# Halving the columns that each level of a triangular inverse multiplies, copies and merges, in a diffusion trunk with PEER experts on one core

## The chip, the core and the metric

One NeuronCore of a Trainium2 chip. The metric is the device time of one execution of the program in microseconds (us), where less is better. Durations below are us unless marked ns. The engines are PE (TensorE: MATMUL, with its weight loads LDWEIGHTS listed as PEld), DVE (VectorE), ACT (ScalarE), POOL (GpSimd) and SP (SyncE, which only issues DMAs here).

## The reference, cut to what matters

One inference step of two trunk layers, over 128 context tokens and 256 latent tokens. A layer has an input projection, four mixers side by side (a state space scan, a gated delta rule, a Fourier mixer, windowed attention), an output projection, and then PEER experts: every token picks 128 of 16,384 experts, and each expert is one row of 1,024 numbers in a table U and one in a table V, gathered from HBM.

The part that the change touches is the triangular solve of the gated delta rule:

```python
kk = jnp.einsum('bchid,bchjd->bchij', kc, kc)
A = jnp.where(strict, bc[..., :, None] * kk * decay, 0.0)
rhs = jnp.concatenate([vc * bc[..., None], kc * (bc * jnp.exp(gcum))[..., None]], axis=-1)
sol = lax.linalg.triangular_solve(jnp.eye(CHUNK, dtype=A.dtype) + A, rhs,
                                  left_side=True, lower=True)
```

All of it is fp32.

## The kernel before

**Tiles and units.** Tokens lie in three tiles of 128. The work is four units in this order: the context tile in layer 0 (one tile), the two latent tiles in layer 0, the context tile in layer 1, the two latent tiles in layer 1. Each unit runs its stages in a fixed order (norm, proj, intra for each tile, scan, fnet, attention, out, query, topk). The stage `st_intra(u, i)` holds the solve of one tile, so it runs six times: once, twice, once, twice.

**The inverse.** For each of two directions `d` (forward and backward) and four heads the kernel inverts a 128 x 128 unit triangular matrix by doubling. X and its transpose XT begin as the inverse of the 2 x 2 diagonal blocks. At level `lv` (1 to 6) blocks of 2^lv rows are joined to blocks of twice that size: P = N X (`inner`, L778), copied from PSUM to SBUF by ACT (L1284), then X gets the product of XT and P, and XT the product of P and XT (`outer`, L785), but only at the places that the level fills. The other places are kept by a mask: DVE merges the PSUM result into X (L1650) and XT (L1653) by `copy_predicated` under a mask of the level. The four heads of a direction share a PSUM bank of 512 columns: banks 0 and 1 take P, 2 and 3 X, 4 and 5 XT. At the last level X isn't needed, so it has no X product. The stationary operand (lhsT) of each of these matmuls is a 128 x 128 matrix; the moving operand is the second one. A helper `mm` (L565) issues every matmul and `tr` (L568) every transpose; `fn` (L1090) issues every ACT copy. An fp32 matmul appears in the trace as two LDWEIGHTS and two MATMUL instructions. The order on PE in a level is inner(0, lv), outer(1, lv-1), outer(0, lv), inner(1, lv).

**The weave.** Beside the units runs side work, at places written by hand (`SAMPLE_WEAVE`, `FIRST_WEAVE`, `PROMPT_WEAVE`, called by `gap`). In the first unit the side items are `modquad` (PE multiplies two of eight chunks of four weight blocks, which SP loads 1 MB at a time). In later units they are the experts of the unit before: for each of 128 slots POOL gathers 128 rows of a table with one indirect DMA (L542) into a ring of 12 places, and then either DVE multiplies and reduces it (`item_u`, L1967, table U) or PE sums it with weights (`item_v`, table V). An item is four such rows. POOL waits for a place of the ring to be free, DVE or PE wait for the row to land. In the latent units the six levels of an intra stage have items of the U kind between the merges of direction 0 and those of direction 1: one at each level of the first tile, and at all but one level of the second. In the context unit of layer 1 they have V items, two at each level. After the last unit the last experts run alone. The gathers go in one fixed order.

Of the kernel before, what the change touches and what calls it, by code (L numbers as in the profile page):

```python
# [27 lines left out]
P = 128  # L28
# [239 lines left out]
def build(nc, a, outs, seen):  # L268
# [11 lines left out]
    with ExitStack() as ctx:  # L280
# [5 lines left out]
        def sem(name):  # L286
            if name not in sems:
                sems[name] = ctx.enter_context(nc.semaphore(name))
            return sems[name]

        def tick(name, key=0, by=1):

            s = SEMAPHORE_OF.get(name, name)
            counts[s] = counts.get(s, 0) + by
            noted[name, key] = counts[s]
            return sem(s), by
# [25 lines left out]
        lvl = sb("lvl", [P, 2, LEVELS, P], mybir.dt.uint8)  # L322
# [68 lines left out]
        pb = ctx.enter_context(nc.psum_tensor("pb", [P, 6, 512], F32))  # L391
# [9 lines left out]
        def bc1(ap, n):  # L401

            return ap.unsqueeze(1).to_broadcast((ap.shape[0], n) + tuple(ap.shape[1:]))
# [14 lines left out]
        def big_at(o, *shape):  # L418
            n = int(np.prod(shape))
            v = big[:, o:o + n]  # L420
            if len(shape) == 2:
                return v.rearrange("p (a b) -> p a b", b=shape[1])
            if len(shape) == 3:
                return v.rearrange("p (a b c) -> p a b c", b=shape[1], c=shape[2])
            return v

        rows_in = [sem(f"rows_in{j}") for j in range(RING)]
        rows_used = [sem(f"rows_used{j}") for j in range(RING)]
        wcol_ready = sem("wcol_ready")
# [122 lines left out]
        def _(pe):  # L552
# [3 lines left out]
            def take(banks, until):  # L556


                for b in banks:
                    if b in held:  # L560
                        pe.wait_ge(*done(*held[b]))
                    held[b] = until

            def mm(out, lhsT, rhs, start=True, stop=True):
                return nc.tensor.matmul(out, lhsT, rhs, start=start, stop=stop)  # L565
# [169 lines left out]
            def st_intra(u, i):  # L735
                g, l, nt, NC, c0 = dims(u)
                t0 = slice(i * P, i * P + P)
                for d in range(2):
                    pe.wait_ge(*done("summands_ready", (u, i, d)))
                    take([2 * d, 2 * d + 1], ("dec_ready", (u, i, d)))  # L740
                    for m in range(2):
                        mm(pb[:, 2 * d + m, :], ones, big[:, d * 1024 + m * 512:d * 1024 + m * 512 + 512], stop=False)
                        for h in range(4):
                            last = mm(pb[:, 2 * d + m, h * P:h * P + P], ident, con("negm", d, P), start=False, stop=h == 3)
                    last.then_inc(*tick("rows_full", (u, i, d)))
                take([4, 5], ("cb_read", (u, i)))
                for gr in range(2):
                    s = slice(64 * gr, 64 * gr + 64)
                    last = mm(pb[:, 4 + gr, 0:P], cv[s, 2, t0], cv[s, 3, t0])
                last.then_inc(*tick("cb_full", (u, i)))  # L750
                gap(u, f"intra{i}", 0)
                for base, qk in ((0, 6), (2, 4)):
                    take([base, base + 1], ("kk_read" if base == 0 else "qk_read", (u, i)))
                    for h in range(HEADS):
                        s = slice(64 * (h % 2), 64 * (h % 2) + 64)
                        last = mm(pb[:, base + h % 2, h // 2 * P:h // 2 * P + P], cv[s, 6 + h // 2, t0], cv[s, qk + h // 2, t0])
# [8 lines left out]
                for h in range(HEADS):  # L765
                    for d in range(2):
                        last = mm(pb[:, 0, h * HD:h * HD + HD], big_at(2048 + 512 * d, 4, P)[:, h, :],
                                  big_at(3072 + 256 * d, 4, HD)[:, h, :], start=d == 0, stop=d == 1)
                last.then_inc(*tick("y_full", (u, i)))
                gap(u, f"intra{i}", 2)  # L770
                for d in range(2):
                    pe.wait_ge(*done("xt_ready", (u, i, d, 0)))
                    take([2 + d], ("x0_ready", (u, i, d, 0)))
                    for n in range(4):
                        last = tr(pb[:, 2 + d, n * P:n * P + P], big_at(2048 + 512 * d, 4, P)[:, n, :])
                    last.then_inc(*tick("x_full", (u, i, d, 0)))

                def inner(d, lv):  # L778
                    pe.wait_ge(*done("x_ready" if lv > 1 else "x0_ready", (u, i, d, lv - 1)))
                    take([d], ("p_copied", (u, i, d, lv)))  # L780
                    for n in range(4):
                        last = mm(pb[:, d, n * P:n * P + P], big_at(512 * d, 4, P)[:, n, :], big_at(1024 + 512 * d, 4, P)[:, n, :])
                    last.then_inc(*tick("p_full", (u, i, d, lv)))

                def outer(d, lv):  # L785
                    pe.wait_ge(*done("p_copied", (u, i, d, lv)))
                    pe.wait_ge(*done("xt_ready", (u, i, d, lv - 1)))
                    if lv < LEVELS - 1:
                        take([2 + d], ("x_ready", (u, i, d, lv)))
                        for n in range(4):  # L790
                            last = mm(pb[:, 2 + d, n * P:n * P + P], big_at(2048 + 512 * d, 4, P)[:, n, :],
                                      big_at(3072 + 512 * d, 4, P)[:, n, :])
                        last.then_inc(*tick("x_full", (u, i, d, lv)))
                    take([4 + d], ("xt_ready", (u, i, d, lv)))
                    for n in range(4):
                        last = mm(pb[:, 4 + d, n * P:n * P + P], big_at(3072 + 512 * d, 4, P)[:, n, :],
                                  big_at(2048 + 512 * d, 4, P)[:, n, :])
                    last.then_inc(*tick("xt_full", (u, i, d, lv)))

                for lv in range(1, LEVELS):  # L800
# [13 lines left out]
                for d in range(2):  # L814
                    for h in range(HEADS):
                        last = mm(pb[:, 0, d * 256 + h * HD:d * 256 + h * HD + HD],
                                  big_at(2048 + 512 * d, 4, P)[:, hpos(h), :], big_at(4096 + 256 * d, 4, HD)[:, h, :])
                last.then_inc(*tick("u_full", (u, i)))
                if g:
                    take([1], ("wt_copied", (u, i)))  # L820
                    for d in range(2):
                        for h in range(HEADS):
                            s = slice(64 * (h % 2), 64 * (h % 2) + 64)
                            o = d * 256 + h // 2 * P
                            last = mm(pb[s, 1, o:o + P], big_at(4608 + 256 * d, 4, HD)[:, h, :],
                                      big_at(2048 + 512 * d, 4, P)[:, hpos(h), :])
# [259 lines left out]
        def _(act):  # L1086
            step, stepped = stepper("act_step")

            def fn(out, in_, f=ACT.Copy, **kw):
                return nc.scalar.activation(out, in_, f, **kw)  # L1090
# [176 lines left out]
            def st_intra(u, i):  # L1267
                g, l, nt, NC, c0 = dims(u)
                gap(u, f"intra{i}", 0)
                for d in range(2):  # L1270
                    act.wait_ge(*done("rows_full", (u, i, d)))
                    for m in range(2):
                        for h in range(4):
                            c = m * 8 + d * 4 + h
                            last = fn(dec[:, d, m * 4 + h, :], pb[:, 2 * d + m, h * P:h * P + P], ACT.Exp, bias=sca[:, 10, i, c:c + 1])
                    last.then_inc(*tick("dec_ready", (u, i, d)))
                gap(u, f"intra{i}", 2)
                for d in range(2):
                    act.wait_ge(*done("x_full", (u, i, d, 0)))
                    fn(big_at(1024 + 512 * d, 512), pb[:, 2 + d, :]).then_inc(*tick("x0_ready", (u, i, d, 0)))  # L1280
                for lv in range(1, LEVELS):
                    for d in range(2):
                        act.wait_ge(*done("p_full", (u, i, d, lv)))
                        fn(big_at(3072 + 512 * d, 512), pb[:, d, :]).then_inc(*tick("p_copied", (u, i, d, lv)))  # L1284
                    gap(u, f"intra{i}", 2 + lv)
                act.wait_ge(*done("u_full", (u, i)))
                fn(sol[:, i, :, :], pb[:, 0, :].rearrange("p (a b) -> p a b", b=256)).then_inc(*tick("u_copied", (u, i)))
                if g:
                    act.wait_ge(*done("wt_full", (u, i)))
                    fn(solW[:, i, :], pb[:, 1, :]).then_inc(*tick("wt_copied", (u, i)))  # L1290
# [171 lines left out]
        def _(dve):  # L1462
# [3 lines left out]
            def item_const():  # L1466
                dve.memset(cinP[:, :, :], 0.0)
                dve.memset(cinS[:, :, :], 0.0)
                dve.memset(wcol[:, :, :], 0.0)
                dve.memset(c15[:, :], 15)  # L1470
                dve.memset(epsc[:, :], EPS).then_inc(*tick("init"))  # L1471

# [101 lines left out]
            def st_intra(u, i):  # L1574
# [11 lines left out]
                for d in range(2):  # L1586
                    b = bet[:, i, d * 4:d * 4 + 4].rearrange("p (pair par) -> p par pair", par=2)
# [15 lines left out]
                for d in range(2):  # L1603
                    dve.wait_ge(*done("dec_ready", (u, i, d)))
                    cb = pb[:, 4:6, 0:P]
                    for r in range(2):
                        dst = big_at(2048 + 512 * d, 2, 2, P)[:, :, r, :]
                        src = dec[:, d, 0:4, :].rearrange("p (g r) j -> p g r j", g=2)[:, :, r, :]
                        last = tt(dst, cb, src, ALU.mult)
                last.then_inc(*tick("cb_read", (u, i)))  # L1610
                dve.wait_ge(*done("qk_full", (u, i)))
                for d in range(2):
                    last = tt(attnT[:, i, d, :].rearrange("p (a b j) -> p a b j", a=2, b=2),
                              pb[:, 2:4, 0:256].rearrange("p a (b j) -> p a b j", b=2), heads_by_parity(dec[:, d, 4:8, :]), ALU.mult)
# [21 lines left out]
                for d in range(2):  # L1636
                    xt = big_at(2048 + 512 * d, 4, P)
# [3 lines left out]
                for lv in range(1, LEVELS):  # L1641
                    if lv == LEVELS - 1:
                        right_sides(u, i)
                    for d in range(2):
                        if d and lv < LEVELS - 1:
                            gap(u, f"intra{i}", 2 + lv)
                        x, xt = big_at(1024 + 512 * d, 4, P), big_at(2048 + 512 * d, 4, P)
                        if lv < LEVELS - 1:
                            dve.wait_ge(*done("x_full", (u, i, d, lv)))
                            dve.copy_predicated(x, bc1(lvl[:, 1 - d, lv, :], 4), pb[:, 2 + d, :].rearrange("p (a b) -> p a b", b=P)) \  # L1650
                                .then_inc(*tick("x_ready", (u, i, d, lv)))
                        dve.wait_ge(*done("xt_full", (u, i, d, lv)))
                        dve.copy_predicated(xt, bc1(lvl[:, d, lv, :], 4), pb[:, 4 + d, :].rearrange("p (a b) -> p a b", b=P)) \  # L1653
                            .then_inc(*tick("xt_ready", (u, i, d, lv)))
                gap(u, f"intra{i}", 1 + LEVELS)
                gap(u, f"intra{i}", 9)
# [403 lines left out]
```

## Time and profile before

| | |
|---|---|
| time, median of 3 runs (lowest to highest) | 2727.9 us (2726.73 to 2729.89) |
| the profiled execution | 2733.57 us |
| its span, from first to last instruction | 2731.8 us |
| mean granted TensorE clock over the span | 0.816 |
| busy: PE, PEld, DVE, ACT, POOL | 1789.8, 1096.3, 1645.4, 379.2, 1455.8 |
| HBM read | 955.11 MB, 350 GB/s over the span |
| indirect gathers on POOL | 1536 |

PE busy and PEld busy overlap, since a weight load runs beside the matmul before it. [...] An idle engine costs nothing by itself; what counts is which wait ends last in a stage. The span is cut by the view of stretches, where an x behind a busy time counts instructions that touch the stretch.

### The profile page before, as it was taken

The page shows a single profiled execution, that of the slowest core. Times are in us where ns is not written, and L with a number is a line of the kernel's source. Part 1 is how long each engine was busy: PE and PEld are TensorE (multiplying, and loading weights), DVE is VectorE, ACT ScalarE, POOL GpSimd, SP SyncE. Part 2 cuts the span into 40 slices and gives each one's busy share as a digit, 9 for nine tenths or more (in the row PEclk, how much of TensorE's full clock was granted, in tenths as well). Part 3 has the DMA queues.
Part 4 walks back from the last instruction along what each step waited for, and adds up shares of the span by engine and source line. Part 5 has one row for each costly group of instructions (what it writes and reads, how often), then busy time and mean ns, then how long its engine had stood idle before and what let it go on. Part 6 is the DMA issues. An engine that isn't in the chain of part 4 may idle for free. (4 is left out here: it accounts for less than half of the span.)

```text
span 2731.8 us, 28087 instructions
## 1 busy us (share of the span) xinstructions
PE 1789.8 (66%) x10274; PEld 1096.3 (40%) x10274; DVE 1645.4 (60%) x4093; ACT 379.2 (14%) x903; POOL 1455.8 (53%) x1540
## 2 busy tenths in 40 slices
PE   6988688768994111089888797767992000088888
PEld 5857567646643111054253386655650000011111
DVE  2526898871589898942116488882299999900000
ACT  3222231111111000011111132112110000000000
POOL 0000553332667676767765544333466777777775
PEclk9989798868996555589999898867996555599999
DMA  9487796656999999999999897656899999999998
GB/s 396 163 338 291 291 407 206 210 200 231 374 416 416 420 420 420 420 372 417 408 421 420 321 381 281 207 195 206 335 408 381 420 420 420 420 420 419 395 419 342
DMA packets 249208, 959.36 MB, mean 351 GB/s; under 512 B 32368, under 2 KB 33648, under 8 KB 231280
## 3 DMA queue, kind: packets, MB, share of 16 engines
q0 software_dynamic: 221184, 805.40, 74.6%
q1 hardware_dynamic: 19584, 142.62, 13.0%
q10 hardware_dynamic: 8304, 9.56, 1.0%
q8 instruction: 82, 1.34, 0.2%
q14 instruction: 54, 0.44, 0.0%
HBM read 955.11 MB, written 2.36 MB: 350 GB/s over the span
## 5 line engine op out<-in xcount | busy, mean ns | idle before, releaser
L542 POOL DMA_INDIRECT sb_ring<-in_peer_u,sb_idxu x768 | 726.6, 946 | 775.0 <-DVE sb_idxT L1935 287.7
L542 POOL DMA_INDIRECT sb_ring<-in_peer_v,sb_idxT x768 | 728.9, 949 | 478.7 <-PE pv L565 214.1
L1967 DVE CUSTOM_DVE_ANT_0 sb_ring<-sb_ring,pv 128x1024 f32<-128x1024 f32 x768 | 906.3, 1218 | 33.3 <-DMA sb_ring<-in_peer_u,sb_idxu 25.1
L565 PE MATMUL pv<-sb_ring,sb_wcol 128*32 128x512 f32 x3072 | 653.8, 626 | 74.8 <-DMA sb_ring<-in_peer_v,sb_idxT 63.0
L565 PE MATMUL pb<-sb_hT,sb_wring 128*128 128x256 f32 (+1 forms) x1920 | 375.6, 356 | 49.2 <-ACT sb_big L1090 26.7
L565 PEld LDWEIGHTS pb<-sb_hT,sb_wring 128*128 128x128 f32 x1920 | 321.5, 203 | 123.1 <-issue 70.0
L565 PEld LDWEIGHTS pv<-sb_ring,sb_wcol 128*32 128x32 f32 x3072 | 125.3, 111 | 541.7 <-DMA sb_ring<-in_peer_v,sb_idxT 365.5
L568 PE MATMUL pb<-sb_cst,sb_dots 128*128 128x128 f32 x6 | 2.4, 401 | 416.1 <-DVE sb_dots L1973 416.1
L565 PE MATMUL pb<-sb_big 128*128 128x128 f32 (+2 forms) x1888 | 244.9, 296 | 32.0 <-DVE sb_big L1650 22.7
L565 PEld LDWEIGHTS pb<-sb_big 128*128 128x128 f32 (+1 forms) x1888 | 233.1, 205 | 53.9 <-DVE sb_big L1650 29.7
L1981 DVE COPY sb_accv<-pv 128x512 f32<-128x512 f32 x12 | 8.3, 690 | 342.2 <-PE pv L565 337.7
L565 PE MATMUL pb<-sb_big,sb_cst 128*128 128x256 f32 (+6 forms) x304 | 100.2, 506 | 129.7 <-ACT sb_cinP L1090 45.0
L568 PEld LDWEIGHTS pb<-sb_cst,sb_dots 128*128 128x128 f32 x6 | 1.0, 160 | 418.1 <-DVE sb_dots L1973 418.1
L1090 ACT ACTIVATE sb_big<-pb 128x512 f32<-128x512 f32 (+3 forms) x184 | 84.1, 466 | 524.4 <-PE pb L565 442.6
L565 PEld LDWEIGHTS pb<-sb_big,sb_cst 128*128 128x128 f32 (+2 forms) x304 | 53.5, 231 | 148.9 <-ACT sb_big L1090 73.1
L565 PE MATMUL pb<-sb_wring,sb_hT 128*128 128x256 f32 x352 | 82.1, 392 | 26.7 <-DVE sb_cv L1512 26.7
L1836 DVE SCALAR_TENSOR_TENSOR sb_xT<-pb,sb_modT,sb_xT 128x128 f32<-128x128 f32 (+1 forms) x32 | 13.4, 417 | 137.5 <-PE pb L565 137.5
L1650 DVE COPY_PREDICATED sb_big<-sb_lvl,pb 128x512 f32<-128x512 uint8 x60 | 43.5, 726 | 83.4 <-PE pb L565 83.4
L1843 DVE MAX8 sb_xe<-sb_dec 128x8 f32<-128x128 f32 x128 | 27.9, 280 | 103.8 <-ACT sb_cv L1090 64.0
L565 PEld LDWEIGHTS pb<-sb_wring,sb_hT 128*128 128x128 f32 x352 | 68.8, 197 | 37.7 <-issue 28.0
L1090 ACT ACT_TABLE_LOAD x54 | 69.3, 1283 | 6.2 <-DVE sb_epsc L1471 3.7
L1967 DVE DVE_READ_ACCUMULATOR2_ANT sb_dots<- 128x1 f32 x768 | 63.6, 83 | 0.0
(234 smaller groups left out, 1662.3 us busy)
## 6 DMA issues: line engine op xcount, KB each, us to landing
sb_ring<-in_w_mod_blocks SPq DMA_DIRECT2D x38, 1024.0 KB, 8.2
sb_wring<-in_w_in_blocks SPq DMA_DIRECT2D x34, 1024.0 KB, 7.7
sb_wring<-in_w_q_blocks SPq DMA_DIRECT2D x26, 1024.0 KB, 8.5
sb_wring<-in_w_out_blocks SPq DMA_DIRECT2D x14, 1024.0 KB, 7.7
sb_ring<-in_peer_u,sb_idxu POOLq DMA_INDIRECT x768, 9.2
sb_ring<-in_peer_v,sb_idxT POOLq DMA_INDIRECT x768, 8.0
sb_wring<-in_w_mod_blocks SPq DMA_DIRECT2D x10, 1024.0 KB, 7.7
sb_ring<-in_w_in_blocks SPq DMA_DIRECT2D x6, 1024.0 KB, 17.3
```

Of the source, the lines that this page charges most:

```text
L542: pool.indirect_dma_start(ring[:, j, :], None, a["tab_" + kind][l_of(q)], bass.IndirectOffsetOnAxis(ap=of, axis=0)).then_inc(rows_in[j], 16)
L565: return nc.tensor.matmul(out, lhsT, rhs, start=start, stop=stop)
L568: return nc.tensor.transpose(out, in_, ident[0:in_.shape[0], 0:in_.shape[0]])
L1090: return nc.scalar.activation(out, in_, f, **kw)
L1650: dve.copy_predicated(x, bc1(lvl[:, 1 - d, lv, :], 4), pb[:, 2 + d, :].rearrange("p (a b) -> p a b", b=P)) \
L1836: stt(x, pb[:, 4 + j % 2, 0:NC], modT[:, l, 16 + j, g:g + 1], x, ALU.mult, ALU.add) \
L1843: last = dve.max(vals(r)[:, lo:lo + 8], rows(r))
L1967: dve.tensor_tensor_reduce(out=row, in0=row, in1=pv[:, :, :].rearrange("p a b -> p (a b)"), scale=1.0, scalar=0.0, op0=ALU.mult, op1=ALU.a ...
L1981: dve.tensor_copy(accv[:, :], pv[:, k, :]).then_inc(*tick("v_summed", (q, k)))
```

## The change

Of the 128 columns of a head, a level can change only those whose bit `lv` is 1 (for X of direction 0), or 0 (for its transpose), and the other way round for direction 1. The change takes these 64 columns as a strided view (runs of 2^lv columns, 2^lv apart), and has `inner` and `outer` use them as moving operand, with results of 64 columns a head packed into the first 256 columns of the bank. ACT writes P into the same places of its tile, DVE merges 256 columns in place of 512. As P is read in full as the stationary operand of the XT product, one memset clears the half of its tile that might never have been written. The waits, the order and the number of instructions in the levels stay. The whole diff:

```diff
--- before.py
+++ after.py
@@ -423,6 +423,14 @@
             if len(shape) == 3:
                 return v.rearrange("p (a b c) -> p a b c", b=shape[1], c=shape[2])
             return v
+
+        def bit_columns(ap, lv, bit):
+
+            return ap.rearrange("p n (b two r) -> p n b two r", two=2, r=1 << lv)[:, :, :, bit, :]
+
+        def halves_of(bank, lv):
+
+            return bank.rearrange("p (n b r) -> p n b r", n=4, r=1 << lv)
 
         rows_in = [sem(f"rows_in{j}") for j in range(RING)]
         rows_used = [sem(f"rows_used{j}") for j in range(RING)]
@@ -778,8 +786,9 @@
                 def inner(d, lv):
                     pe.wait_ge(*done("x_ready" if lv > 1 else "x0_ready", (u, i, d, lv - 1)))
                     take([d], ("p_copied", (u, i, d, lv)))
+                    x = bit_columns(big_at(1024 + 512 * d, 4, P), lv, d)
                     for n in range(4):
-                        last = mm(pb[:, d, n * P:n * P + P], big_at(512 * d, 4, P)[:, n, :], big_at(1024 + 512 * d, 4, P)[:, n, :])
+                        last = mm(halves_of(pb[:, d, 0:256], lv)[:, n], big_at(512 * d, 4, P)[:, n, :], x[:, n])
                     last.then_inc(*tick("p_full", (u, i, d, lv)))
 
                 def outer(d, lv):
@@ -787,14 +796,14 @@
                     pe.wait_ge(*done("xt_ready", (u, i, d, lv - 1)))
                     if lv < LEVELS - 1:
                         take([2 + d], ("x_ready", (u, i, d, lv)))
+                        p = bit_columns(big_at(3072 + 512 * d, 4, P), lv, d)
                         for n in range(4):
-                            last = mm(pb[:, 2 + d, n * P:n * P + P], big_at(2048 + 512 * d, 4, P)[:, n, :],
-                                      big_at(3072 + 512 * d, 4, P)[:, n, :])
+                            last = mm(halves_of(pb[:, 2 + d, 0:256], lv)[:, n], big_at(2048 + 512 * d, 4, P)[:, n, :], p[:, n])
                         last.then_inc(*tick("x_full", (u, i, d, lv)))
                     take([4 + d], ("xt_ready", (u, i, d, lv)))
+                    xt = bit_columns(big_at(2048 + 512 * d, 4, P), lv, 1 - d)
                     for n in range(4):
-                        last = mm(pb[:, 4 + d, n * P:n * P + P], big_at(3072 + 512 * d, 4, P)[:, n, :],
-                                  big_at(2048 + 512 * d, 4, P)[:, n, :])
+                        last = mm(halves_of(pb[:, 4 + d, 0:256], lv)[:, n], big_at(3072 + 512 * d, 4, P)[:, n, :], xt[:, n])
                     last.then_inc(*tick("xt_full", (u, i, d, lv)))
 
                 for lv in range(1, LEVELS):
@@ -1281,7 +1290,8 @@
                 for lv in range(1, LEVELS):
                     for d in range(2):
                         act.wait_ge(*done("p_full", (u, i, d, lv)))
-                        fn(big_at(3072 + 512 * d, 512), pb[:, d, :]).then_inc(*tick("p_copied", (u, i, d, lv)))
+                        fn(bit_columns(big_at(3072 + 512 * d, 4, P), lv, d), halves_of(pb[:, d, 0:256], lv)) \
+                            .then_inc(*tick("p_copied", (u, i, d, lv)))
                     gap(u, f"intra{i}", 2 + lv)
                 act.wait_ge(*done("u_full", (u, i)))
                 fn(sol[:, i, :, :], pb[:, 0, :].rearrange("p (a b) -> p a b", b=256)).then_inc(*tick("u_copied", (u, i)))
@@ -1467,6 +1477,7 @@
                 dve.memset(cinP[:, :, :], 0.0)
                 dve.memset(cinS[:, :, :], 0.0)
                 dve.memset(wcol[:, :, :], 0.0)
+                dve.memset(big_at(3584, 512), 0.0)
                 dve.memset(c15[:, :], 15)
                 dve.memset(epsc[:, :], EPS).then_inc(*tick("init"))
 
@@ -1647,10 +1658,12 @@
                         x, xt = big_at(1024 + 512 * d, 4, P), big_at(2048 + 512 * d, 4, P)
                         if lv < LEVELS - 1:
                             dve.wait_ge(*done("x_full", (u, i, d, lv)))
-                            dve.copy_predicated(x, bc1(lvl[:, 1 - d, lv, :], 4), pb[:, 2 + d, :].rearrange("p (a b) -> p a b", b=P)) \
+                            dve.copy_predicated(bit_columns(x, lv, d), bit_columns(bc1(lvl[:, 1 - d, lv, :], 4), lv, d),
+                                                halves_of(pb[:, 2 + d, 0:256], lv)) \
                                 .then_inc(*tick("x_ready", (u, i, d, lv)))
                         dve.wait_ge(*done("xt_full", (u, i, d, lv)))
-                        dve.copy_predicated(xt, bc1(lvl[:, d, lv, :], 4), pb[:, 4 + d, :].rearrange("p (a b) -> p a b", b=P)) \
+                        dve.copy_predicated(bit_columns(xt, lv, 1 - d), bit_columns(bc1(lvl[:, d, lv, :], 4), lv, 1 - d),
+                                            halves_of(pb[:, 4 + d, 0:256], lv)) \
                             .then_inc(*tick("xt_ready", (u, i, d, lv)))
                 gap(u, f"intra{i}", 1 + LEVELS)
                 gap(u, f"intra{i}", 9)
```

## Rows read from the trace of the kernel before

**Rows 1.** The page: busy shares and instructions; granted clock, in 40 equal slices.

```profile
PE 1789.8 (66%) x10274; PEld 1096.3 (40%) x10274; DVE 1645.4 (60%) x4093; ACT 379.2 (14%) x903; POOL 1455.8 (53%) x1540
...
PEclk9989798868996555589999898867996555599999
```

**Rows 2.** Stretches: PE, PEld, DVE, ACT, POOL; clock; DMA. Six inverses, then the tail.

```profile
99.40:137.80 38.40, 38.30 (x375) 33.89 (x373) 17.67 (x28) 8.53 (x15) 0.00 (x0) 1.00 0.42 167
417.80:461.40 43.60, 36.19 (x273) 33.87 (x272) 38.24 (x68) 7.77 (x13) 18.73 (x20) 0.93 0.70 236
495.90:535.70 39.80, 33.99 (x274) 32.05 (x272) 33.99 (x59) 7.76 (x13) 15.00 (x16) 0.97 0.60 203
1197.50:1257.60 60.10, 59.53 (x464) 37.71 (x464) 17.69 (x28) 8.32 (x20) 45.13 (x49) 1.00 1.02 417
1670.20:1713.90 43.70, 36.27 (x274) 33.94 (x272) 38.26 (x68) 7.76 (x13) 18.73 (x20) 0.93 0.69 231
1748.40:1787.80 39.40, 33.59 (x274) 31.76 (x272) 33.52 (x59) 7.76 (x13) 14.98 (x16) 0.98 0.59 199
...
2068.00:2731.00 663.00, 292.20 (x1088) 58.46 (x1080) 324.57 (x553) 12.30 (x44) 478.90 (x511) 0.74 1.00 408
```

**Rows 3.** Timeline of DVE, one level of the first latent tile, layer 0.

```profile
428.72 0.72 DVE L1650 COPY_PREDICATED sb_big<-sb_lvl,pb 128x512 f32<-128x512 uint8 x1
429.33 0.72 DVE L1653 COPY_PREDICATED sb_big<-sb_lvl,pb 128x512 f32<-128x512 uint8 x1
...
431.16 1.21 DVE L1967 CUSTOM_DVE_ANT_0 sb_ring<-sb_ring,pv 128x1024 f32<-128x1024 f32 x1
...
435.72 0.72 DVE L1650 COPY_PREDICATED sb_big<-sb_lvl,pb 128x512 f32<-128x512 uint8 x1
```

**Rows 4.** Timeline of PE, the same inverse; brackets hold the idle time before.

```profile
415.55 1.12 PE L568 MATMUL pb<-sb_cst,sb_big 128*128 128x128 f32 x4 [2.37 <-DVE sb_big L1640]
...
429.50 5.95 PE L565 MATMUL pb<-sb_big 128*128 128x128 f32 x48 [1.33 <-DVE sb_big L1650]
436.50 5.96 PE L565 MATMUL pb<-sb_big 128*128 128x128 f32 x48 [1.05 <-DVE sb_big L1650]
```

**Rows 5.** Waits in the same inverse: total, times, longest.

```profile
POOL sb_ring L542 <- DVE sb_dots L1967: 28.3, 10, 17.4
```

**Rows 6.** Timeline of PE: the pace of narrow and wide matmuls.

```profile
93.40 1.89 PE L565 MATMUL pb<-sb_big 128*128 128x64 f32 x16
...
110.77 5.62 PE L565 MATMUL pb<-sb_big 128*128 128x128 f32 x48
...
417.79 4.26 PE L565 MATMUL pb<-sb_big 128*128 128x128 f32 x19
...
1817.15 4.69 PE L565 MATMUL pb<-sb_sol,sb_hT 128*128 128x64 f32 x21
```

**Rows 7.** Stretches of PE alone: PE busy, clock, DMA.

```profile
417.80:419.80 2.00, 2.00 (x11) 0.50 0.00 0
...
421.80:423.80 2.00, 2.00 (x18) 0.97 0.00 0
...
1816.90:1818.90 2.00, 1.99 (x10) 0.50 0.04 8
1818.90:1820.90 2.00, 2.00 (x11) 0.50 0.15 18
1820.90:1822.90 2.00, 2.00 (x11) 0.50 0.84 268
```

**Rows 8.** Groups by line and shape: count, busy, mean ns, idle before.

```profile
L1640 DVE TENSOR_TENSOR sb_big<-sb_big,sb_cst 128x512 f32<-128x512 f32 x12 | 8.3, 692 | 0.4
...
L1668 DVE TENSOR_TENSOR sb_big<-sb_tok,sb_bet 128x256 f32<-128x256 f32 x12 | 5.1, 425 | 0.4
```

**Rows 9.** Timeline of PE, first context tile, before its inverse.

```profile
97.66 0.66 PE L568 MATMUL pb<-sb_cst,sb_big 128*128 128x128 f32 x4 [1.37 <-DVE sb_big L1640]
98.99 0.66 PE L568 MATMUL pb<-sb_cst,sb_big 128*128 128x128 f32 x4 [0.67 <-DVE sb_big L1640]
```

## Prediction

> **What bounds the kernel now.** I read the page first. [...] After 2068 us only experts run, with the DMA engines full (share 1.00); nothing of the change lies there. The six inverses are 99.4 to 137.8, 417.8 to 461.4, 495.9 to 535.7, 1197.5 to 1257.6, 1670.2 to 1713.9 and 1748.4 to 1787.8 [rows 2]. Each has 272 matmul instructions of its own: 34 products (12 P, 10 X, 12 XT), four heads, two instructions each.
>
> They have three different bounds. In the first, PE is busy for 38.30 of 38.40 us. In the fourth (context tile, layer 1) DMA share is 1.02 and POOL issues 49 gathers in 60.1 us, one each 1.23 us: the rows set the pace. In the other four, the latent tiles, neither does: DMA share is 0.59 to 0.70, and POOL waited 28.3 us in one of them for DVE to free a place of the ring [rows 5], so rows lie ready. From level 2 on DVE runs without a pause: a level from merge to merge takes 7.0 us (428.72 to 435.72), of which four merges take 2.44 (one each 0.61) and four expert rows 4.56 (1.14 each) [rows 3]; PE needs 5.95 us for its 48 instructions and idles 1.05 [rows 4]. As rows wait for the work there, what these four inverses gain or lose should arrive at the end of the kernel in full.
>
> **The change part by part.**
>
> *Matmuls, 1,632 instructions with 64 columns in place of 128.* At the high clock 48 instructions of 128 columns take 5.62 us, 0.117 each; 16 of 64 columns take 1.89, 0.118 each. At the low clock 19 of 128 columns take 4.26 (0.224), 21 of 64 take 4.69 (0.223) [rows 6]. The two extra ones cost 0.43, so the pace at the low clock is 0.214. [...] So PE gains nothing while the clock is the same.
>
> *Merges.* 512 elements become 256, with more strides. Pace of a merge now 0.61; between like operations of DVE, 256 elements take 0.425 and 512 take 0.692, 0.27 less [rows 3, 8]. I take 0.34. Bounds: 0.61, if strided masks and runs of two columns cost what the halving saves, and 0.30, half of all. Of the 132 merges the 88 in the latent tiles count where DVE is the bound, 23 us at most by 0.27 each.
>
> *P copies on ACT.* ACT is busy 7.8 of 43.6 us with 13 copies of 0.6 [rows 2], and all but the last lie under another product: 0. Without that cover half of a copy, 0.3, would be the gain of each. *The memset*, about 0.7 us of DVE by the 512-element rows, lies in the start-up while weights land: 0, at most 0.7.
>
> *The clock.* This is the term that decides. PE would get the same number of instructions but stream half the columns. Look at what came before the clock rose and where it didn't. At 417.8 us the inverse begins at the low clock; PE is full with 128-column matmuls, and from 421.8 the clock is at 0.97. From 1816.9 to 1822.9 PE is just as full with 64-column ones, and it stays at 0.50 through all of it [rows 7]. The busy share is the same; only the columns differ. All four latent inverses begin low: their mean clock is 0.93 to 0.98, against 1.00 in the first and fourth [rows 2], because PE pauses 2.37 us for DVE before them. The eight transposes of 128 columns that follow are all the wide work left [rows 4]. In the changed kernel nothing in these inverses streams 128 columns any more, so I expect the low clock to last to their end. Then PE is the bound: 272 x 0.214 = 58.2, and 0.7 for the last wait on a copy of P, 58.9 each. Against 43.6, 39.8, 43.7 and 39.4 [rows 2] that is 15.3 + 19.1 + 15.2 + 19.5 = **+69 us**. DVE's 2.44 or 1.4 of merges and 4.56 of rows fit below a PE level of 48 x 0.214 = 10.3. After the last of them the next 32 narrow matmuls also start low: +1. The last merges before the right sides are multiplied are shorter, 0.5 in each of five inverses: -2.
>
> [...]
>
> *First inverse.* It begins at the high clock and PE is full, also with 16 `modquad` instructions between levels. Same pace, same time, less 0.5 (in the -2 above). Bound on the other side: if it falls low, 272 x (0.214 - 0.117) = 26, and seven modquads at 1.0 us more each.
>
> *Fourth inverse.* 10 us a level by the rows; PE fills about 5.6 of it with the inverse and has V rows, which stream 512 columns, for the rest. A fall of the clock should mend itself there. 0, bounds -1 and +5.
>
> **Sum.** +69 + 1 - 2 = +68. The profiled execution took 2733.57 us for a span of 2731.8; the median of three is 2727.9, 0.2% below it. I add to the median: 2796 us.
>
> **The rivals.**
>
> *The clock holds, and it gets faster.* Were the clock to rise in the latent inverses as now, DVE would be the bound with 4.56 + 4 x 0.34 = 5.9 a level in place of 7.0, just what PE needs (48 x 0.117 = 5.6). PE's idle time there, 1.05 to 1.33 a level [rows 4], is all there is to gain: 5 us in the first tile of a unit, 4 in the second, where one level has no rows. 18 in all and 1 elsewhere: 2709 us. It decides if narrow matmuls raise the clock. For it: once high, the clock stayed at 1.00 in whole inverses with PE idle 1 of 7 us. Against it: the stretch at 1817 us. The chance is 0.10.
>
> *The matmuls cost by their columns.* Half the time on PE: the first inverse would drop by some 15 us (272 x 0.058) and the latent ones by the 18 that DVE allows: 2695. [...] Rows 6 speak against it where every matmul has its own load. 0.03.
>
> *The first inverse falls low too.* PE pauses 1.37 and 0.67 us ahead of its transposes, at the high clock, and in this execution the clock lived through that [rows 9]. If it doesn't, the old kernel would recover in the next wide matmuls and lose little; the new one might not. +26 + 7: 2829. 0.25.
>
> *The clock comes back halfway in some of them.* About half of the 69: 2762. 0.08.
>
> *Nothing reaches the end*, because rows or weights were late anyway, or the low clock costs and the merges' gain cancel: 2728. Against it: POOL's waits [rows 5]. 0.04.
>
> **How the numbers follow.** The main case has 0.50. Slower is main case, first inverse low, and halfway: 0.83. Same is 0.04, faster is 0.13. Within 0.2% (5.5 us) is what a measurement of this kernel can't tell from no change; its three runs lie 3.2 us apart. The range takes in the main case with its bounds, the first inverse low, and halfway: 2758 to 2836; it leaves out the gains and no change, 0.17.
>
> **What would show it.** In the changed kernel's profile: the 64-column matmuls at 0.21 us from start to start in the latent inverses, and granted clock 0.50 over nearly all of them; each of those inverses near 59 us, DVE idle in it; merges near 0.34 us apart where they follow each other, at most 0.45 long; the first inverse 38 us and the fourth 60 as now, at 1.00. The tail after the last topk should be as long as now. The prediction is wrong if the latent inverses show the clock at 1.00 with narrow matmuls (then it is a gain), if narrow matmuls start less than 0.1 us apart, or if the inverses grow and the end doesn't move.

## The result: 76 us slower, and the profile after

The changed kernel takes 2804.47 us (median of 4 runs, 2799.2 to 2806.56), the kernel before beside it 2728.89 (2726.73 to 2731.7). The ratio is 1.0262, 95% interval 1.0239 to 1.0285. The forecast was 2796 us in a range of 2758 to 2836. A ratio, here and below, is not the quotient of the two medians: it leaves out runs that count as slow, over 1.5% above the fastest of the same kernel, while medians are of all runs. The profiled execution took 2806.12 us with a span of 2804.3 (before: 2733.57 and 2731.8).

The page first: busy shares, and the strip of the granted clock. They answer to [rows 1].

```profile
PE 1880.5 (67%) x10274; PEld 1196.4 (43%) x10274; DVE 1619.5 (58%) x4094; ACT 364.3 (13%) x903; POOL 1455.7 (52%) x1540
...
PEclk8989795557997656589999895656997555589999
```

PE streams fewer columns and is busy for 91 us more. DVE is busy for 26 less.

Now the stretches of the six inverses and of the tail, columns as in [rows 2]: PE, PEld, DVE, ACT, POOL; clock; DMA.

```profile
103.30:141.10 37.80, 37.80 (x374) 33.81 (x372) 12.59 (x27) 6.00 (x15) 0.00 (x0) 1.00 0.43 167
423.90:482.70 58.80, 58.33 (x273) 57.96 (x272) 34.94 (x67) 5.23 (x13) 18.73 (x20) 0.50 0.54 179
515.20:574.00 58.80, 58.33 (x273) 57.99 (x272) 30.39 (x59) 5.23 (x13) 14.99 (x16) 0.50 0.42 144
1239.30:1300.30 61.00, 60.34 (x464) 37.74 (x464) 12.57 (x27) 5.67 (x19) 45.66 (x49) 1.00 1.02 418
1712.50:1771.40 58.90, 58.40 (x274) 58.02 (x272) 34.94 (x67) 5.23 (x13) 18.73 (x20) 0.50 0.53 179
1802.90:1861.70 58.80, 58.33 (x273) 57.98 (x272) 30.37 (x59) 5.23 (x13) 14.98 (x16) 0.50 0.42 143
2140.50:2803.50 663.00, 292.13 (x1084) 58.66 (x1076) 324.57 (x552) 12.35 (x44) 478.70 (x511) 0.74 1.00 408
```

All four latent inverses run at clock 0.50 from end to end, with PE and its weight loads busy for 58 of these us, and take 58.8 to 58.9 us against 43.6, 39.8, 43.7 and 39.4. That is 69 us. The first (37.8 for 38.4) and the fourth (61.0 for 60.1) are at 1.00 and as they were. In the tail of 663 us PE and POOL are busy to within 0.2 us as long as in [rows 2].

The timeline of PE in the first latent inverse answers to [rows 4]. Before, there was a pause of 1.05 to 1.33 us in each level; here there is none for 264 instructions.

```profile
423.03 1.03 PE L576 MATMUL pb<-sb_cst,sb_big 128*128 128x128 f32 x4 [0.67 <-DVE sb_big L1651]
423.86 56.42 PE L573 MATMUL pb<-sb_big 128*128 128x64 f32 x264
480.75 1.97 PE L573 MATMUL pb<-sb_big 128*128 128x64 f32 x8 [0.47 <-ACT sb_big L1099]
```

56.42 us for 264 is 0.214 each. The timeline of DVE in one level (to set beside [rows 3]) shows the bound's other side: a merge of 256 elements is 0.43 long, but now it waits 1.28 for PE, and the next expert row has to wait with it.

```profile
444.47 0.43 DVE L1661 COPY_PREDICATED sb_big<-sb_lvl,pb 128x256 f32<-128x256 uint8 x1
446.18 0.43 DVE L1665 COPY_PREDICATED sb_big<-sb_lvl,pb 128x256 f32<-128x256 uint8 x1 [1.28 <-PE pb L573]
447.88 0.42 DVE L1661 COPY_PREDICATED sb_big<-sb_lvl,pb 128x256 f32<-128x256 uint8 x1 [1.28 <-PE pb L573]
449.59 0.43 DVE L1665 COPY_PREDICATED sb_big<-sb_lvl,pb 128x256 f32<-128x256 uint8 x1 [1.28 <-PE pb L573]
449.93 1.21 DVE L1980 CUSTOM_DVE_ANT_0 sb_ring<-sb_ring,pv 128x1024 f32<-128x1024 f32 x1
...
454.71 0.43 DVE L1661 COPY_PREDICATED sb_big<-sb_lvl,pb 128x256 f32<-128x256 uint8 x1
```

A level of 7.0 us (merge to merge) became 10.2 (444.47 to 454.71).

The rest of the 72.5 us of span, 3.7, is what is left of shifts both ways. When the first latent inverse begins, the execution is already 6.1 us behind the one before (423.9 for 417.8). Of these, 3.9 were there before the first inverse began (103.3 for 99.4). They aren't the change's: over the eleven profiles of this case that start lies at 98.9 to 103.3, and kernels with and without narrow matmuls stand at both ends. Then 2.8 come between the first inverse and the first latent one. On the other side, the stretches between the two latent inverses of a unit take 32.5 and 31.5 us, where they took 34.5 each.

These stretches of PE alone (PE busy, clock, DMA) follow the first inverse, where the 2.8 begin:

```profile
139.80:143.20 3.40, 2.87 (x30) 1.00 1.01 426
143.30:150.00 6.70, 6.70 (x47) 0.50 0.43 176
150.00:153.50 3.50, 3.50 (x18) 0.50 0.05 10
```

Before, the clock was high without a break from 139 to 152 us; here, after narrow matmuls with a pause of 0.53, it is low from 143.3. It needn't be: in the kernel that merges twice (below), with the same matmuls in this unit and a pause of 1.31 there, PE is at 1.00 from 138.3 to 150.

### The profile page after: what moved, and what is told of

It is laid out like the page before. It is cut to its first block, busy times and chain, and to the rows that moved or that the text cites. A ratio compares the mean times of both kernels' runs of the same rounds, so it can differ in the third digit from the quotient of the medians.

```text
span 2804.3 us, 28088 instructions
## 1 busy us (share of the span) xinstructions
PE 1880.5 (67%) x10274; PEld 1196.4 (43%) x10274; DVE 1619.5 (58%) x4094; ACT 364.3 (13%) x903; POOL 1455.7 (52%) x1540
## 4 chain that ended last, share of the span: by engine, by line
PE 30%; POOL 26%; DVE 19%; DMA 12%; issue 10%; ACT 2%; ACTq 0%; SPq 0%; POOLq 0%; DVEq 0%
POOL sb_ring L550 26%; PE pb L573 25%; DVE sb_ring L1980 7%; PE pv L573 5%; DMA sb_ring<-in_peer_v,sb_idxT 5%; DMA sb_ring<-in_peer_u,sb_idxu 5%; DMA sb_wring<-in_w_in_blocks 1%; DVE sb_i16u L1860 1%; DVE sb_big L1527 1%; PE pb L576 1%; ACT sb_big L1099 1%; ACT sb_hT L1099 1%; DMA sb_ring<-in_w_mod_blocks 1%; DVE sb_xe L1856 1%; DMA sb_wring<-in_w_mod_blocks 1%
## 5 line engine op out<-in xcount | busy, mean ns | idle before, releaser
L573 PE MATMUL pb<-sb_big 128*128 128x64 f32 (+1 forms) x1888 | 336.9, 370 | 6.2 <-DVE sb_big L1665 3.2
L573 PEld LDWEIGHTS pb<-sb_big 128*128 128x128 f32 (+1 forms) x1888 | 332.2, 281 | 20.3 <-issue 8.0
L1099 ACT ACTIVATE sb_big<-pb 128x256 f32<-128x256 f32 (+3 forms) x184 | 69.0, 383 | 609.3 <-PE pb L573 526.7
L1661 DVE COPY_PREDICATED sb_big<-sb_lvl,pb 128x256 f32<-128x256 uint8 x60 | 29.4, 489 | 116.5 <-PE pb L573 114.6
L1665 DVE COPY_PREDICATED sb_big<-sb_lvl,pb 128x256 f32<-128x256 uint8 x72 | 34.9, 485 | 68.8 <-PE pb L573 68.8
```

What stands on the lines that cost most here:

```text
L1661: dve.copy_predicated(bit_columns(x, lv, d), bit_columns(bc1(lvl[:, 1 - d, lv, :], 4), lv, d), halves_of(pb[:, 2 + d, 0:256], lv)) \
L1665: dve.copy_predicated(bit_columns(xt, lv, 1 - d), bit_columns(bc1(lvl[:, d, lv, :], 4), lv, 1 - d), halves_of(pb[:, 4 + d, 0:256], lv)) \
```

## Experiments

Two theories were to be told apart. **Clock theory**: a 64-column matmul costs what a 128-column one costs at the same clock, but PE full of them can't raise the clock from 0.50 (low) to 1.00 (high); the loss is all in the four latent inverses. **View theory**: the strided operands, packed results or many short runs are slow in themselves. Chips differ between the three groups of runs below (the kernel before took 2931.14 us in the first, 2729.41 in the second, 2732.3 in the third), so only ratios to the kernel before of the same group are compared, and stretches.

### Where the loss is: latent units alone, context units alone

```diff
+        def narrow(u, lv):
+            return u % 2 == 1
...
-                    x = bit_columns(big_at(1024 + 512 * d, 4, P), lv, d)
+                    x, out = big_at(1024 + 512 * d, 4, P), pb[:, d, :].rearrange("p (a b) -> p a b", b=P)
+                    if narrow(u, lv):
+                        x, out = bit_columns(x, lv, d), halves_of(pb[:, d, 0:256], lv)
```

and so in the X and XT products, the copy of P and the merges: where `narrow` is false they are those of the kernel before. This is latent_only; context_only has `u % 2 == 0` (the context units).

> The change in the two latent units only (four of the six inverses); the context units as in the kernel before. Clock theory: all of the +70 comes from here, 2795 to 2802 us. Rival (strided views cost in every inverse alike): four sixths of the loss, about 2779 us.

> The change in the two context units only. Clock theory: these inverses start at the high clock and keep it, so 2728 to 2734 us; a few us of loss can come from the stretch after the first inverse, where the clock fell at 143 us in the changed kernel. Rival (strided views cost everywhere): two sixths of the loss, about 2753 us.

Latent units alone: 2994.76 us against 2931.14, ratio 1.0197 (1.0164 to 1.0230); the medians differ by 64 us, and the ratio on 2931.14 gives 58. Context units alone: 2939.86, ratio 1.0025 (0.9991 to 1.0059), 9 us by the medians and 7 by the ratio. So the loss is in the latent units. It is 58 to 64 and not the +70 expected, and by itself the first run doesn't decide: its interval is 48 to 67 us, with the rival's four sixths (51) inside and +70 outside. The second run does: the rival asked for 25 us there, and the interval ends at 17. On this chip the gathers are slower (414 in the 600 us from 2380, near its end, against 511 in 663 us in [rows 2]), which may hide a part of it; that wasn't tried. The traces show the loss itself in full: the latent inverses take 58.9 us here too. Stretches of latent_only, its second and fourth inverse:

```profile
427.60:486.50 58.90, 58.38 (x273) 58.00 (x272) 34.98 (x68) 5.23 (x13) 18.72 (x20) 0.50 0.53 179
1277.40:1348.50 71.10, 65.54 (x466) 39.88 (x464) 17.33 (x27) 8.40 (x19) 43.89 (x48) 1.00 0.95 348
```

Context_only showed a second thing. Its profiled execution took 2971.57 us, and its first inverse was this:

```profile
100.90:172.30 71.40, 71.38 (x374) 62.87 (x372) 12.49 (x27) 6.01 (x15) 0.00 (x0) 0.50 0.30 118
```

71.4 us at the low clock (0.50) where other executions take 38 at the high one (1.00). That is the third rival of the prediction, in some executions and not in others: 3 of the 10 runs of this kernel were above 2966, the other 7 between 2925.63 and 2945.57.

### The changed kernel once more

> The changed kernel itself, so that the others of this group have it beside them on one chip. Clock theory: ratio to the kernel before 1.022 to 1.030, the four latent inverses 58.9 us each at the low clock. In some executions the first inverse falls low too, which would show as times some 33 us higher.

Median 2832.68 us, ratio 1.0291 (1.0237 to 1.0344). The ratio leaves out the two highest runs; the medians' quotient is 1.038. The six runs fall into two lots: 2793.82 and 2800.53, and four from 2831.06 to 2843.98. The profiled one, 2831.06, is of the second, and its first two inverses are

```profile
100.80:172.20 71.40, 71.37 (x374) 62.87 (x372) 12.50 (x27) 6.01 (x15) 0.00 (x0) 0.50 0.30 118
454.10:513.00 58.90, 58.40 (x274) 58.02 (x272) 34.95 (x67) 5.24 (x13) 18.73 (x20) 0.50 0.53 179
```

The first inverse low costs 71.4 - 37.8 = 33.6 us, and the latent ones are as in the first measurement. So the changed kernel has two times, about 2800 and about 2835. That they go by the clock at which its first inverse begins is read from one profile of either kind, on two chips. The mean granted clock of each run fits: 0.784 and 0.782 in the two low times, 0.766 to 0.773 in the four high ones, 0.781 and 0.782 in the first measurement.

### The same views, each column streamed twice

```diff
-                    x = bit_columns(big_at(1024 + 512 * d, 4, P), lv, d)
+                    x = twice(bit_columns(big_at(1024 + 512 * d, 4, P), lv, d))
                     for n in range(4):
-                        last = mm(halves_of(pb[:, d, 0:256], lv)[:, n], big_at(512 * d, 4, P)[:, n, :], x[:, n])
+                        last = mm(doubles_of(pb[:, d, :], lv)[:, n], big_at(512 * d, 4, P)[:, n, :], x[:, n])
```

and the same for X and XT. `twice` repeats the view by a broadcast dimension, `doubles_of` holds both copies of the result, and ACT and DVE read the first.

> The changed kernel, with the same strided views, packed results, half P copies and half merges; but every matmul streams its 64 columns twice in a row (128 moving columns, the second 64 results are not used). Clock theory: the streamed columns are all that mattered, so the clock rises again and the latent inverses take 37 to 42 us; ratio to the kernel before 0.993 to 1.000. Rival (strided views or packed halves are slow): no better than the changed kernel, 1.022 to 1.030, or worse by the added columns.

**2705.33 us (2701.67 to 2709.02) against 2729.41, ratio 0.9907 (0.9890 to 0.9924).** Twice the columns on PE, everything else as in the changed kernel but for the distance between the heads' results in PSUM, and a loss of 2.6 to 2.9% is a gain of 0.9%, 24 us. The ratio is better than the best that was expected (0.993), and the inverses lie at the lower end of the expected 37 to 42 us or below it. Its latent inverses:

```profile
414.50:452.50 38.00, 34.12 (x273) 32.67 (x272) 33.04 (x67) 5.25 (x13) 18.72 (x20) 0.95 0.72 255
483.10:520.20 37.10, 33.71 (x273) 32.45 (x272) 28.90 (x59) 5.24 (x13) 14.99 (x16) 0.95 0.60 209
1653.90:1691.70 37.80, 33.92 (x273) 32.50 (x272) 33.01 (x67) 5.24 (x13) 18.74 (x20) 0.96 0.73 255
1724.30:1760.40 36.10, 32.69 (x273) 31.44 (x272) 28.90 (x59) 5.23 (x13) 14.99 (x16) 0.98 0.61 212
```

The clock is at 0.95 to 0.98 again, for 0.50 in the changed kernel. The view theory falls here: strided operands, and results packed within each head, are all still there, and the inverses take 36.1 to 38.0 us for 58.8 to 58.9.

The first merge of the second direction in level 1, and two of level 2 (start, duration):

```profile
425.19 0.72 DVE L1669 COPY_PREDICATED sb_big<-sb_lvl,pb 128x256 f32<-128x256 uint8 x1
...
431.54 0.42 DVE L1669 COPY_PREDICATED sb_big<-sb_lvl,pb 128x256 f32<-128x256 uint8 x1
431.87 0.43 DVE L1673 COPY_PREDICATED sb_big<-sb_lvl,pb 128x256 f32<-128x256 uint8 x1
```

In level 1, the one whose runs are two columns, a merge of 256 elements is as long as one of 512 was (0.72 in [rows 3]). From level 2 on it is mostly 0.43.

### Wide matmuls, half merges

```diff
-dve.copy_predicated(x, bc1(lvl[:, 1 - d, lv, :], 4), pb[:, 2 + d, :].rearrange("p (a b) -> p a b", b=P))
+dve.copy_predicated(bit_columns(x, lv, d), bit_columns(bc1(lvl[:, 1 - d, lv, :], 4), lv, d),
+                    bit_columns(pb[:, 2 + d, :].rearrange("p (a b) -> p a b", b=P), lv, d))
```

This is against the kernel before; XT likewise, matmuls and P copies untouched. Only DVE's work is halved.

> Matmuls and P copies as in the kernel before (128 columns a head), but DVE merges only the 256 columns that a level can change, reading them strided from PSUM. Clock theory (narrow matmuls don't raise the clock, merges are cheaper): the clock rises in the latent inverses as before, granted clock 0.93 to 0.98 there, merges lie 0.34 to 0.42 apart where nothing is waited for, a level takes 5.9 to 6.3 us in place of 7.0, the four latent inverses take 34 to 39.5 us, and the whole about 2710 us (2704 to 2718). Rival (the strided views are what costs): merges are no cheaper, 2728 us or more.

> The kernel of wide matmuls and half merges once more, on a chip whose kernel before is nearer 2728 us. It differs from the one that streams its columns twice in reading PSUM in strides and copying P in full. If the merges' half is all the gain there: ratio 0.989 to 0.993, as that one's. If strided PSUM reads or the full copies cost something: 0.993 to 0.998, as in its first measurement.

On the slow chip of the first group: 2924.43 us, ratio 0.9966 (0.9948 to 0.9985), half of the gain expected; its latent inverses take 38.5 to 41.3 us there, and why was not followed up. Third group: 2705.93 us (2701.38 to 2709.92) against 2732.3, **ratio 0.9901 (0.9881 to 0.9922)**, the same as with columns streamed twice. So the gain on DVE that the first rival counted is real, it is independent of the narrow matmuls, and neither strided reads of PSUM nor the full copy of P takes it away. Two of its latent inverses, for the 43.6 and 39.8 of [rows 2]:

```profile
418.60:456.80 38.20, 34.33 (x273) 32.88 (x272) 33.24 (x67) 7.76 (x13) 18.73 (x20) 0.95 0.73 257
487.20:524.60 37.40, 33.92 (x274) 32.66 (x272) 29.12 (x59) 7.76 (x13) 15.00 (x16) 0.95 0.61 207
```

Like the one that streams twice it beats both kernels, and it is simpler.

Its first inverse shows what the kernels with narrow matmuls lack. Here too it begins at the low clock (stretches of PE alone: PE busy, clock, DMA):

```profile
102.50:104.50 2.00, 2.00 (x11) 0.50 0.03 8
104.50:106.50 2.00, 2.00 (x18) 0.90 0.00 0
```

With wide matmuls the clock is back in the second stretch (0.90), and the 32 matmuls of its beginning take 4.89 us for 3.79 in kernels that begin it high: 1.1 us lost, where narrow ones lost 33.6.

### Only level 1 wide

`narrow` is `lv > 1`: level 1 has wide matmuls with half merges, levels 2 to 6 are as changed.

> As the changed kernel, but level 1 of each inverse has 128-column matmuls; levels 2 to 6 stay narrow. Clock theory: the wide level raises the clock as in the kernel before and the narrow ones keep it, so the latent inverses show a granted clock above 0.9 and take 34 to 40 us, the whole is 2704 to 2722 us. Rival (narrow strided matmuls are slow by themselves): only a sixth of the loss is gone, about 2790 us. Between the two, if the clock falls back under narrow matmuls in some inverses: 2730 to 2780 us.

2972.22 us, ratio 1.0127 (1.0088 to 1.0166), 41 us by the medians and 37 by the ratio. The main expectation was missed; it is the third case named, in which the clock falls back under narrow matmuls. The latent inverses take 53 us each. Three stretches of the first (level 1, the start of level 2, the rest):

```profile
427.70:437.80 10.10, 10.09 (x74) 9.82 (x72) 5.32 (x9) 2.17 (x4) 1.92 (x3) 0.82 0.09 17
439.10:441.50 2.40, 2.38 (x21) 2.38 (x22) 2.40 (x6) 0.73 (x2) 0.83 (x1) 1.00 0.88 287
441.60:480.60 39.00, 38.50 (x180) 38.12 (x179) 25.40 (x51) 2.68 (x7) 14.98 (x16) 0.50 0.68 236
```

The wide level did raise the clock. Then PE paused 1.33 us for DVE and its four expert rows, as it does in the kernel before [rows 4], and went on with narrow matmuls; the clock was at 1.00 through the pause and for over 2 us behind it, then fell and stayed at 0.50 for the rest. Wide matmuls after the same pause kept it up (1.00 from 429.5 to 435.5 in the kernel before). In the first inverse of this and the changed kernel's first measurement, narrow matmuls kept it up as well (1.00). That stage differs in two ways: it has no such pauses, and between its levels stand 16 `modquad` instructions of 256 columns.

### The same, with the pauses filled

```diff
                 def inner(d, lv):
+                    if g and d and lv > 1:
+                        for _ in range(3 if lv == 2 else 1):
+                            mm(pb[:, 1, 256:512], ident, cst[:, 0:256])
```

> Narrow matmuls from level 2 on, wide ones in level 1, and in the latent inverses one matmul of 256 columns a level (three at level 2) whose result nobody reads, placed where PE waits for DVE. It only adds work to PE. Clock theory: without it the clock fell in PE's 1.3 us pause at level 2 and each inverse took 53 us; with it the clock stays high and they take 38 to 43 us; ratio to the kernel before 0.995 to 1.004. Rival (narrow matmuls can't hold the clock up in these stages, whatever fills the pause): 53 us an inverse or more, ratio 1.012 to 1.018.

2711.14 us (2701.63 to 2723.06), ratio 0.9939 (0.9919 to 0.9960), a little better than expected. (Without the filler the clock fell some 2.5 us after the pause, not in it as expected above.) The profiled execution is the fastest of the six; the others have a mean granted clock of 0.810 to 0.815 where it has 0.822, so they may have lost the clock somewhere. The profiled execution's timeline of PE over two levels:

```profile
422.61 1.51 PE L577 MATMUL pb<-sb_cst 128*128 128x256 f32 x6
424.12 5.57 PE L577 MATMUL pb<-sb_big 128*128 128x64 f32 x48
429.52 0.65 PE L577 MATMUL pb<-sb_cst 128*128 128x256 f32 x2
430.17 5.57 PE L577 MATMUL pb<-sb_big 128*128 128x64 f32 x48
```

The inverse took 37.9 us at a mean clock of 0.95. Fourteen useless PE instructions took 15 us off it. Its 48 narrow instructions take 5.57 us where 48 wide ones take 5.62 [rows 6]: at the same clock they cost the same. So narrow matmuls can hold the clock up in these stages. Whether the end of the pause does it or the 256 columns of the filler isn't shown: a filler of narrow matmuls wasn't run.

### Every merge twice

Each merge is done a second time, behind the first and waiting for it; its result is the same:

```diff
+                            merge(x, 1 - d, 2 + d, lv, d).then_inc(*step())
+                            dve.wait_ge(*stepped())
                             last = merge(x, 1 - d, 2 + d, lv, d)
```

> The changed kernel with every merge done twice, the second behind the first (it writes the same values): 88 more merges in the latent units at 0.4 to 0.5 us each. Clock theory: DVE is idle for 4 us of each level there, so hardly anything moves: latent inverses 58.9 to 61 us, ratio to the kernel before as the changed kernel's, 1.02 to 1.035 (which end depends on the first inverse's clock, 38 or 71 us). Rival (narrow merges are on the path): 35 to 44 us more than the changed kernel, ratio 1.037 or more.

2810.78 us against 2732.3, ratio 1.0322 (1.0267 to 1.0377); the interval overlaps the changed kernel's 1.0237 to 1.0344. The ratio alone is wide: one of the four runs took 2843.7, the others 2801.85 to 2815.64. The inverse says it better:

```profile
415.90:474.90 59.00, 58.53 (x274) 58.13 (x272) 44.50 (x88) 5.22 (x13) 18.74 (x20) 0.50 0.53 178
```

DVE is busy 44.5 us in place of 34.9, and the inverse takes 59.0 for 58.9. In the changed kernel what DVE does in the latent inverses costs nothing; PE, busy 58.5 of the 59.0 us at clock 0.50, hides it.

## Why the prediction was right

- **Which stretches matter.** Right. Tail, fourth inverse and (in the first measurement) first inverse are unchanged; latent units alone carry the loss.
- **Matmuls cost the same with half the columns.** Right: 0.214 measured at the low clock (0.50) for 264 of 64 columns in a row, as worked out from [rows 6], and 5.57 us for 48 at the high one (1.00), against 5.62 with 128 columns. What sets this pace was not shown: the weight loads are busy for 57.96 of the 58.8 us, but no run of these stages had a smaller load.
- **The clock.** Right, and the term that decides, though it was read from one stretch of 6 us: 58.9 expected for each latent inverse, 58.8 to 58.9 measured, +69 us. Streaming the columns twice gives it all back (36.1 to 38.0 each), which shows that it is the columns and not the views. That PE's pause of 2.37 us is why the latent inverses begin low was my estimate, and in the trace of the kernel before it holds for two of the four at most: ahead of the second and the fourth the clock is at 0.50 already before that pause, from 484 to 490 and from 1738 to 1742 us.
- **Merges.** 0.34 apart was close: in the kernel that streams twice, four of them start 0.33 to 0.34 apart. The bound of 0.45 on their length holds for most of them from level 2 on, also where they wait for PE. It failed in level 1: four of 22 merges of an inverse take 0.71 to 0.77, so that the mean is 0.49. There two start 0.52 apart (425.19 and 425.71 us), nearer to my upper bound of 0.61, by which strides and runs of two columns cost what the halving saves. I had the first rival's gain at 19 us; with the clock kept up, 24 and 26 us were measured. The latent inverses hold 17 us of the 24, for the 18 that I had. It is the 1 elsewhere that was too small: the stretches between the two latent inverses of a unit take 30.6 and 32.6 us in place of 34.5, 6 us in all, at a mean clock of 0.83 and 0.76 for 0.65. In both, the 32 narrow matmuls behind the inverse take 3.02 us; before, they took 5.58.
- **Sum.** +68 was 8 below the measured +76. The span, which the terms were read from, grew by 72.5; the other 3 are the distance of the two profiled executions from their medians. The +69 was met, and the -1 of the rest came out as +3.7. No term of mine was 3.9 late before the first inverse, which is scatter between executions. I saw a fall of the clock within the first inverse as a rival, but not one just behind it, where the low stretch from 143.3 to 153.5 us goes with the 2.8 that follow; and I had nothing for the shorter stretches between latent inverses. So the nearness of 2796 is in part luck: parts that I didn't see cancel.
- **Rivals.** "The clock holds" is refuted for this kernel; once the clock is held, its price is right in the inverses and short by 5 elsewhere. "By their columns" is refuted by the 5.57 us for 5.62. "The first inverse falls low" happened in the second measurement: 71.4 us where I had 38.4 + 33, and totals from 2831 where I had 2829. The total agrees by luck, as that is another chip. I gave it 0.25 as if it were a property of the kernel; it is one of the execution, with both seen. "Nothing reaches the end" fell to the latent-only kernel.

## What to carry to other kernels

Here each matmul brings its own weight load of 128 x 128 (272 in an inverse), and cutting its moving columns from 128 to 64 saved 0.05 us in 48 instructions (5.57 for 5.62), while it cost the high clock in four stages (0.50 for 0.93 to 0.98). In such a case look in the trace for what PE did before the granted clock rose or fell, and price a change at both clocks, here 0.117 and 0.214 us a matmul. Split a change that helps two engines into its halves; here DVE's half was worth 1% and PE's half cost 3 to 4% (1.026 and 1.029 against 0.990). With narrow matmuls, a pause of 1.33 us on PE ended some 2.5 us before the clock fell to 0.50 for 39 us; in the kernel before the clock stayed at 1.00 behind such a pause.

## What was not expected of the hardware

- Work that nobody reads made the kernel faster: with the filler an inverse takes 37.9 us instead of 53, though on PE it adds 14 instructions.
- Narrow matmuls behave differently by where the clock stands: they held it at 1.00 in a first inverse of 37.8 us, lost it after a pause of 1.33 us, and never raised it from 0.50 in 58.9 us of full PE, nor in 71.4 us of the first inverse.
- One and the same kernel can thus have two times, 33.6 us apart, decided in its first 105 us. The kernel before has not: its 11 runs beside it lie between 2721.79 and 2736.43. In the kernel with half merges wide matmuls bring the clock back: it is at 0.50 from 102.5 to 104.5 us and at 0.90 in the 2 us that follow.
- A merge of 256 elements in runs of two columns takes 0.71 to 0.77 us, as long as one of 512 contiguous ones (0.72) or longer; in longer runs it mostly takes 0.43.
